# Gate columns stationary in four column groups, and attention values by pairs of heads, in a two-layer hybrid trunk

## The chip, the cores and the metric

The kernel runs on one core of one Trainium2 chip. The metric is the device time of one execution in microseconds (us), as the median of repeated runs. TensorE multiplies matrices into PSUM, VectorE, ScalarE and GpSimd work on elements, and SyncE issues most of the loads; the engines meet through semaphores.

## What is computed

Two groups of tokens, 512 latent tokens and 128 context tokens (640 in all), pass through the same two layers of width 1024. In each layer they are normalised and modulated, projected by `w_in`, go through three mixers, are projected by `w_out`, and then go through a routed set of 16 experts. Cut to what the change touches:

```python
p = modulated_norm(x, g_norm1[l], sh1, sc1) @ w_in[l]     # 640 x 1024 by 1024 x PROJ_W
glu, q_na, k_na, v_na, dn_qkv, dn_z, dn_ab = split_projection(p)

# dn_ab: the last 16 columns, gates of the delta mixer
ab = dn_ab.reshape(b, t, 4, DN_HEADS)
g = -exp(a_log) * softplus(ab[:, :, 0:2] + dt_bias)
beta = sigmoid(ab[:, :, 2:4])

# attention: 4 heads of 64; latent tokens see the latent grid (with a bias) and 128 cached context tokens
pr = softmax(concatenate([s_loc, s_ctx], axis=-1), axis=-1)
o = pr @ v          # context tokens see only context
```

All arrays are fp32.

## The kernel before

The kernel is written by hand: each engine has its own program, in the order in which the code is written, and every hand-over is a wait for a count on a semaphore (`need`). Activations lie transposed, features on the 128 partitions and the 640 tokens along the row: `hT` holds eight such tiles (index `k`). Weights come through a ring of three slots of 2 MB; SyncE loads the next piece into a slot when TensorE's last reader of that slot is done (`ring_load`, L518).

**Input projection (L685 to L706).** Seven pieces of `w_in` are worked off. A piece of 512 columns is four products (`gemm`), each of eight steps `k`, and each step of a matmul over 512 tokens (L680) and one over 128 (L681), with 128 weight columns stationary. After the fifth piece (`ci == 4`, the columns called Z) come the 16 gate columns (L704): for each of five blocks of 128 tokens, eight matmuls with the tokens stationary and the 16 weight columns `wab` moving. ScalarE copies them to `ab` (L1338) and makes `beta` (L1340); VectorE makes the gates from `ab` at L1715 to L1721. Then TensorE goes on with the sixth piece (Q and K of the attention, `ci == 5`) and the values of the attention (L692).

**Between projection and attention (L709 to L734).** A layer norm of the convolution mixer runs over TensorE (sums, L714 and L732), ScalarE (L1364, L1376) and VectorE (L1729, L1735, L1738); TensorE also transposes the cached keys, which ScalarE asks for at L1347 after the projection. GpSimd masks the table of attention biases in two operations (L2200, L2202), which VectorE's first attention step (L1753) waits for. In layer 0 GpSimd has stores of zeros (L2187) in its queue ahead of that; they begin when the Z product begins.

**Attention (L737 to L795).** Eighteen rounds: 16 for a block of 128 latent queries and one head, then two for the context tokens with two heads each. In round `i` TensorE transposes the probabilities (`turn_probs`, L760), makes the scores of round `i + 2` (`scores`, L745 and L746), multiplies the probabilities with the values (`values`, L775; L777 for the context rounds), and beside that works off a piece of `w_mod` (modulation for later): `mod_turn` (L639) and `mod_rows` (L633), which has 32 stationary columns in each of four column groups. Layer 0 has twelve such pieces (rounds 1 to 12 load rows, 2 to 13 turn), layer 1 eight. VectorE scales, takes the maximum and normalises (L1753 to L1772), ScalarE takes the exponentials (L1387), copies the transposed probabilities into one of two buffers `pT_` (L1401) and stores the head's result (`att_store`, L1409). A head's 64 outputs go to partitions 0 to 63 or 64 to 127, by the head's parity.

Of the kernel before, what the change touches and what calls it, by code (L numbers as in the profile page):

```python
# [12 lines left out]
P = 128  # L13
# [94 lines left out]
NC = C_SEL + 2  # L108
# [4 lines left out]
def constants():  # L113
# [37 lines left out]
    c[:, C_SEL:C_SEL + 2] = i[:, None] % 32 == np.arange(2)[None, :]  # L151
# [16 lines left out]
def build(nc, x_prompt, x_sample, cache_k, cache_v, state, c, c_ctx, w_mod, b_mod, g1, g2, w_in, conv_w,  # L168
# [11 lines left out]
    with ExitStack() as ctx:  # L180
# [24 lines left out]
        small = sb("small", [P, 1110 + 272])  # L205
# [8 lines left out]
        qkT = work[:, 0:4 * T].rearrange("p (t n) -> p t n", t=4)  # L214
        vna = work[:, 4 * T:4 * T + NCH * NAW].rearrange("p (t n) -> p t n", t=NCH)
# [24 lines left out]
        wab = carve(KD * 16).rearrange("p (k n) -> p k n", k=KD)  # L240
# [125 lines left out]
        ab_done = signal("ab_done", 1)  # L366
        ab_copied = signal("ab_copied", 1)
# [21 lines left out]
        att_o = signal("att_o", 20)  # L389
        att_oc = signal("att_oc", 20)  # L390
# [207 lines left out]
        def _(pe):  # L598
# [20 lines left out]
            for l in range(L):  # L619
# [66 lines left out]
                for ci, (o, w) in enumerate(IN_CHUNKS):  # L686
# [24 lines left out]
                need(ab_copied, 1)  # L711
# [51 lines left out]
                def values(i):  # L763
                    need(att_ptc, i + 1)
                    src = pT_[i % 2]
                    for h in ([i % 4] if i < 16 else [2 * (i - 16), 2 * (i - 16) + 1]):
                        u = i if i < 16 else h + 16
                        r = slice(64 * (h % 2), 64 * (h % 2) + 64)
                        o = ps[r, 3072:3072 + P]
                        if u >= 2:  # L770
                            need(att_oc, u - 1)
                        if i < 16:
                            for j in range(NCH):
                                va = vna[:, j, 64 * h:64 * h + 64] if j < 4 else kvc[1][:, 64 * h:64 * h + 64]
                                ins = mm(o, va, src[:, P * j:P * (j + 1)], start=j == 0, stop=j == NCH - 1)  # L775
                        else:
# [1558 lines left out]
```

## Time and profile before

| | us |
|---|---|
| median of 3 runs | 1985.38 (1984.87 to 1989.67) |
| the profiled execution | 1986.52 |
| its span, first to last instruction | 1984.7 |
| TensorE busy (matmul) | 1726.3 |
| VectorE busy | 856.5 |
| ScalarE busy | 473.9 |
| GpSimd busy | 287.3 |
| mean granted TensorE clock | 0.923 |

The profile is one execution, and its times count from its first instruction. An fp32 matmul shows as two passes, each with its own load of the stationary operand. A row of the timeline merges neighbours of one kind, with their count; in brackets stands the idle time of the engine before it and what ended that. In a row of stretches each engine has its busy time and its count, and behind them stand the granted clock (1.00 is 2.4 GHz, 0.50 is 1.2 GHz), the share of the DMA engines' time that was used, and GB/s.

### The profile page before, as it was taken

The page shows a single profiled execution, that of the slowest core. Times are in us where ns is not written, and L with a number is a line of the kernel's source. Part 1 is how long each engine was busy: PE and PEld are TensorE (multiplying, and loading weights), DVE is VectorE, ACT ScalarE, POOL GpSimd, SP SyncE. Part 2 cuts the span into 40 slices and gives each one's busy share as a digit, 9 for nine tenths or more (in the row PEclk, how much of TensorE's full clock was granted, in tenths as well). Part 3 has the DMA queues.
Part 4 walks back from the last instruction along what each step waited for, and adds up shares of the span by engine and source line. Part 5 has one row for each costly group of instructions (what it writes and reads, how often), then busy time and mean ns, then how long its engine had stood idle before and what let it go on. Part 6 is the DMA issues. An engine that isn't in the chain of part 4 may idle for free. (4 is left out here: it accounts for less than half of the span.)

```text
span 1984.7 us, 22021 instructions
## 1 busy us (share of the span) xinstructions
PE 1726.3 (87%) x8313; PEld 1109.2 (56%) x8313; DVE 856.5 (43%) x1631; ACT 473.9 (24%) x850; POOL 287.3 (14%) x446
## 2 busy tenths in 40 slices
PE   5999996977998895999689999797699989499994
PEld 3555663645887553455355556554488855344553
DVE  2188105556786323111246840254678632411115
ACT  1211003254231213222131110324522120311222
POOL 0000122014442003000211000000435200400002
PEclk9999896988999996999889998798899999699996
DMA  9511996920000106999571101380000010599974
GB/s 344 132 43 65 286 266 210 347 75 1 1 1 1 55 22 260 364 366 362 220 186 68 60 22 43 106 297 1 1 1 1 1 55 21 220 386 360 368 295 180
DMA packets 114392, 302.33 MB, mean 152 GB/s; under 512 B 28000, under 2 KB 36098, under 8 KB 101250
## 3 DMA queue, kind: packets, MB, share of 16 engines
q1 hardware_dynamic: 66576, 221.30, 30.1%
q0 software_dynamic: 14080, 53.48, 8.1%
q10 hardware_dynamic: 33650, 26.37, 4.7%
q8 instruction: 58, 0.95, 0.2%
q14 instruction: 28, 0.23, 0.0%
HBM read 235.04 MB, written 67.05 MB: 152 GB/s over the span
## 5 line engine op out<-in xcount | busy, mean ns | idle before, releaser
L680 PE MATMUL ps<-hreg,ring 128*128 128x512 f32 x768 | 401.7, 605 | 11.1 <-ACT hreg L1291 11.1
L681 PEld LDWEIGHTS ps<-hreg,ring 128*128 128x128 f32 x768 | 148.3, 193 | 188.5 <-issue 188.5
L1124 PE MATMUL ps<-ring,tok 128*128 128x512 f32 x544 | 237.9, 595 | 0.2 <-issue 0.2
L1124 PEld LDWEIGHTS ps<-ring,tok 128*128 128x128 f32 x544 | 103.9, 191 | 130.9 <-issue 130.9
L681 PE MATMUL ps<-hreg,ring 128*128 128x128 f32 x768 | 149.2, 276 | 0.0
L680 PEld LDWEIGHTS ps<-hreg,ring 128*128 128x128 f32 x768 | 119.0, 196 | 11.4 <-issue 11.4
L2126 DVE TENSOR_TENSOR work<-work,ps 128x256 f32<-128x256 f32 x34 | 14.2, 421 | 251.1 <-ACT work L1549 251.1
L1139 PE MATMUL ps<-ring,work 128*128 128x512 f32 x272 | 122.4, 592 | 0.0
L1685 DVE SCALAR_TENSOR_TENSOR mixA<-cin_reg,small,mixA 128x655 f32<-128x655 f32 x120 | 107.1, 896 | 0.0
L2130 DVE COPY zs<-ps 128x1024 f32<-128x1024 f32 x34 | 41.6, 1225 | 120.8 <-PE ps L1139 120.8
L2209 POOL TENSOR_TENSOR hreg<-dnT,cst 128x512 f32<-128x512 f32 x16 | 20.4, 1276 | 488.7 <-DVE dnT L1887 488.7
L1699 DVE SCALAR_TENSOR_TENSOR tmp_reg<-mixb_reg,small,tmp_reg 128x642 f32<-128x642 f32 x96 | 84.7, 882 | 0.0
L1139 PEld LDWEIGHTS ps<-ring,work 128*128 128x128 f32 x272 | 49.1, 191 | 48.8 <-issue 48.8
L2304 POOL DMA_INDIRECT hreg<-ys,slots x10 | 12.5, 1248 | 402.2 <-ACTq L1570 399.8
L1108 PE MATMUL ps<-cst,tok 128*128 128x128 f32 x304 | 43.8, 291 | 27.1 <-DMA tok<-hx,idx 27.1
L1045 PE MATMUL ps<-dnT,ring 128*128 128x512 f32 x128 | 65.5, 594 | 0.0
L1981 DVE SCALAR_TENSOR_TENSOR xT<-ps,small,xT 128x512 f32<-128x512 f32 x16 | 12.0, 751 | 105.9 <-PE ps L1046 105.9
L1326 ACT ACTIVATE mixb_reg<-ps 128x512 f32<-128x512 f32 x24 | 14.3, 598 | 174.0 <-PE ps L681 174.0
L1108 PEld LDWEIGHTS ps<-cst,tok 128*128 128x128 f32 x304 | 39.7, 196 | 28.0 <-issue 25.4
L1717 DVE SCALAR_TENSOR_TENSOR small<-small 128x40 f32<-128x40 f32 x2 | 1.9, 956 | 114.7 <-ACT small L1355 114.7
L1540 ACT ACTIVATE tok<-ps 128x1024 f32<-128x1024 f32 x38 | 38.9, 1025 | 51.7 <-PE ps L1108 48.0
L633 PE MATMUL ps<-ring,small 128*32 128x512 f32 x384 | 47.3, 614 | 3.8 <-issue 2.1
(351 smaller groups left out, 3003.4 us busy)
## 6 DMA issues: line engine op xcount, KB each, us to landing
ring<-in_w SPq DMA_DIRECT2D x102, 1024.0 KB, 7.6
ring<-in_w_mod SPq DMA_DIRECT2D x24, 2048.0 KB, 8.3
ring<-in_w_in SPq DMA_DIRECT2D x12, 2048.0 KB, 8.5
ys<-zs ACTq DMA_DIRECT2D x34, 512.0 KB, 7.7
tok<-xs SPq DMA_DIRECT2D x30, 512.0 KB, 10.7
xs<-zero POOLq DMA_DIRECT2D x8, 1792.0 KB, 19.7
ys<-zero POOLq DMA_DIRECT2D x8, 1664.0 KB, 18.6
ring<-in_w_out SPq DMA_DIRECT2D x4, 2048.0 KB, 7.9
```

The costliest lines, as they stand in the source:

```text
L633: ins = mm(bank(bnk)[32 * j:32 * j + 32], condT[:, k, :], w[:, k, :], start=k < 4, stop=k >= 4)
L680: mm(o[:, 0:TS], lhs(k), rhs(k)[:, 0:TS], start=k == 0, stop=k == nk - 1)
L681: ins = mm(o[:, TS:T], lhs(k), rhs(k)[:, TS:T], start=k == 0, stop=k == nk - 1)
L1045: mm(gslot(gg % 2)[:, 0:TS], lhs, mix(k)[0], start=k == 0, stop=k == KD - 1)
L1108: ins = turn(ps[:, a + P * k:a + P * (k + 1)], xg[q].rearrange("p (m k) -> p k m", k=KD)[:, k], ident)
L1124: ins = mm(bank(2 + q), xgT[q][:, k, :], w, start=k == 0, stop=k == KD - 1)
L1139: ins = mm(bank(4 + 2 * q + n), hidT[:, P * f:P * (f + 1)], ring[2][:, 2048 * q + D * f + 512 * n:2048 * q + D * f + 512 * n + 512], start ...
L1540: A_(xgT[q], ps[:, a:a + D].rearrange("p (k n) -> p k n", k=KD), ACT.Copy).then_inc(xg_copied.sem, 1)
L1685: last[t] = count(V.scalar_tensor_tensor(mixA[:, t, :], src, w, mixA[:, t, :], ALU.mult, ALU.add))
L1699: ins = V.scalar_tensor_tensor(out, src, w, out, ALU.mult, ALU.add)
L2130: V.tensor_copy(ysb[q], ps[:, 2048 + 1024 * q:3072 + 1024 * q]).then_inc(y_out.sem, 1)
L2209: G.tensor_tensor(rcos[t % 2], dnT[:, qk_tile(t), 0:TS], cst[:, C_COS:C_COS + TS], ALU.mult).then_inc(rope_cos.sem, 1)
```

## The change

Three things change.

The gate columns: the padded weight columns (16 and 16 zeros) are the stationary operand, in four column groups, and the tokens move. Group `k % 4` holds the sum over two of the eight steps, so the product lands as four partial sums of 16 rows (each at the start of 32 partitions). ScalarE copies that to `abr` (640 columns). One product later TensorE multiplies each block of 128 tokens of `abr` with a selector of 16 columns, which adds the four groups and turns tokens to partitions. `C_SEL` grows from 2 to 16 columns for that.

The values: `values(a)` runs for two heads at once, in rounds 1, 3, 5 and so on, and its matmuls alternate between partitions 0 to 63 and 64 to 127. One signal and one ScalarE store of 128 partitions serve both heads.

The order within a round: the modulation rows come straight after the scores, then the modulation's turns, then the values.

```diff
-NC = C_SEL + 2
+NC = C_SEL + 16
...
-    c[:, C_SEL:C_SEL + 2] = i[:, None] % 32 == np.arange(2)[None, :]
+    c[:, C_SEL:C_SEL + 16] = i[:, None] % 32 == np.arange(16)[None, :]
...
+        abr = work[:, 4 * T:5 * T]
...
-        wab = carve(KD * 16).rearrange("p (k n) -> p k n", k=KD)
+        wab = carve(KD * 32).rearrange("p (k n) -> p k n", k=KD)
...
                     for m in range(4):
+                        if ci == 5 and m == 1:
+                            need(pT_ready, 1)
+                            need(ab_copied, 1)
+                            for t in range(NCH):
+                                ins = mm(ps[:, 3584 + 16 * t:3600 + 16 * t], abr[:, t * P:(t + 1) * P], cst[:, C_SEL:C_SEL + 16],
+                                         start=True, stop=True)
+                            ins.then_inc(ab_done.sem, 1)
...
                     if ci == 4:
-                        need(pT_ready, 1)
-                        for t in range(NCH):
+                        for a, b in ((0, TS), (TS, T)):
                             for k in range(KD):
-                                ins = mm(ps[:, 3584 + 16 * t:3600 + 16 * t], hT[:, k, t * P:(t + 1) * P], wab[:, k, :],
-                                         start=k == 0, stop=k == KD - 1)
+                                j = 32 * (k % 4)
+                                ins = mm(ps[j:j + 32, 2048 + a:2048 + b], wab[:, k, :], hT[:, k, a:b], start=k < 4, stop=k >= 4)
                         ins.then_inc(ab_done.sem, 1)
...
+                def values(a):
+
+                    halves = [ps[64 * x:64 * x + 64, 3072:3072 + P] for x in range(2)]
+                    if a:
+                        need(att_oc, a)
+                    if a < 8:
+                        need(att_ptc, 2 * a + 2)
+                        for j in range(NCH):
+                            for x in range(2):
+                                h = 2 * (a % 2) + x
                                 va = vna[:, j, 64 * h:64 * h + 64] if j < 4 else kvc[1][:, 64 * h:64 * h + 64]
-                                ins = mm(o, va, src[:, P * j:P * (j + 1)], start=j == 0, stop=j == NCH - 1)
+                                ins = mm(halves[x], va, pT_[x][:, P * j:P * (j + 1)], start=j == 0, stop=j == NCH - 1)
...
-                    values(i)
-
+                    if 1 <= i < 1 + len(beside):
+                        if i >= 2:
+                            pe.wait_ge(mod_copied, beside[i - 2] + 1)
+                        mod_rows(beside[i - 1], 7)
                     if 2 <= i < 2 + len(beside):
+                        need(att_ptc, i + 1)
                         mod_turn(beside[i - 2], later_rows[i % 2], 2688 + 8 * (i - 2))
-                    if 1 <= i < 1 + len(beside):
-                        mod_rows(beside[i - 1], 7)
+                    if i >= 16 or i % 2:
+                        values(i // 2 if i < 16 else i - 8)
...
-                A_(ab, ps[:, 3584:3664].rearrange("p (c n) -> p c n", c=NCH), ACT.Copy).then_inc(ab_copied.sem, 1)
-                need(ab_copied, 1)
-                A_(beta, ab[:, :, 8:16], ACT.Tanh, scale=0.5)\
-                    .then_inc(beta_tanh.sem, 1)
+                A_(abr, ps[:, 2048:2048 + T], ACT.Copy).then_inc(ab_copied.sem, 1)
                 for t in range(4):
                     evac(G_QK + t, qkT[:, t, :]).then_inc(gemm_out[t % 2].sem, 1)
+                    if t == 0:
+                        need(ab_done, 2)
+                        A_(ab, ps[:, 3584:3664].rearrange("p (c n) -> p c n", c=NCH), ACT.Copy).then_inc(ab_copied.sem, 1)
+                        need(ab_copied, 2)
+                        A_(beta, ab[:, :, 8:16], ACT.Tanh, scale=0.5)\
+                            .then_inc(beta_tanh.sem, 1)
...
+                def att_store(a):
+                    need(att_o, a + 1)
+                    h, t = (a % 2, slice((a // 2) * P, (a // 2 + 1) * P)) if a < 8 else (a - 8, slice(TS, T))
+                    A_(mixB[:, h, t], ps[:, 3072:3072 + P], ACT.Copy).then_inc(att_oc.sem, 1)
...
                     if i + 1 < 18:
                         att_probs(i + 1)
+                    if i >= 2 and i % 2 == 0:
+                        att_store(i // 2 - 1)
+                    if i == 17:
+                        att_store(8)
                     att_copy(i)
...
+            V.memset(wab[:, :, 16:32], 0.0)
```

TensorE's program at the end of the Z columns in layer 0, before (`ps` is PSUM, `small` holds `wab`, `hreg` holds `hT`, `ring` the weights; a size is partitions by moving columns):

```order
L680 MATMUL ps<-hreg,ring 128x512
L681 MATMUL ps<-hreg,ring 128x128
L704 MATMUL ps<-small,hreg 128x16 [waits pT_ready]
L704 MATMUL ps<-small,hreg 128x16 x39
L680 MATMUL ps<-hreg,ring 128x512 [waits gemm_out0,ring_loaded2]
L681 MATMUL ps<-hreg,ring 128x128
```

and the same place after the change (`work` holds `abr`, `cst` the selector; "..." stands for the other steps of that product):

```order
L682 MATMUL ps<-hreg,ring 128x128
L712 MATMUL ps<-hreg,small 32x512 x8
L712 MATMUL ps<-hreg,small 32x128 x8
L681 MATMUL ps<-hreg,ring 128x512 [waits gemm_out0,ring_loaded2]
...
L682 MATMUL ps<-hreg,ring 128x128
L702 MATMUL ps<-cst,work 128x16 [waits ab_copied,pT_ready]
L702 MATMUL ps<-cst,work 128x16 x4
L681 MATMUL ps<-hreg,ring 128x512 [waits gemm_out1]
```

Forty matmuls in one run became sixteen, and five more stand behind the first product of the sixth piece.

TensorE's program for rounds 2 and 3 of the attention, before (`hreg` holds probabilities, cached keys and values, `work` Q, K and V, `tmp_reg` the modulation rows):

```order
L760 MATMUL ps<-cst,hreg 128x128 x4
L745 MATMUL ps<-work 128x512 [waits gemm_out0]
L746 MATMUL ps<-hreg,work 128x128
L775 MATMUL ps<-hreg,work 64x128 [waits att_oc,att_ptc]
L775 MATMUL ps<-hreg,work 64x128 x3
L775 MATMUL ps<-hreg 64x128
L639 MATMUL ps<-cst,tmp_reg 128x2 [waits mod_copied]
L639 MATMUL ps<-cst,tmp_reg 128x2 x3
L633 MATMUL ps<-ring,small 32x512 [waits ring_loaded2]
L633 MATMUL ps<-ring,small 32x512 x7
```

which is round 2, and round 3 reads alike. After the change round 2 ends with the turns, and round 3 reads:

```order
L767 MATMUL ps<-cst,hreg 128x128 [waits att_ptc,att_n]
L767 MATMUL ps<-cst,hreg 128x128 x4
L752 MATMUL ps<-work 128x512 [waits gemm_out1]
L753 MATMUL ps<-hreg,work 128x128
L634 MATMUL ps<-ring,small 32x512 [waits ring_loaded0,mod_copied]
L634 MATMUL ps<-ring,small 32x512 x7
L640 MATMUL ps<-cst,tmp_reg 128x2 [waits mod_copied,att_ptc]
L640 MATMUL ps<-cst,tmp_reg 128x2 x3
L781 MATMUL ps<-hreg,work 64x128 [waits att_ptc,att_oc]
L781 MATMUL ps<-hreg,work 64x128 x7
L781 MATMUL ps<-hreg 64x128 x2
```

The values of two rounds stand together, behind the modulation work instead of ahead of it.

## Rows read from the trace of the kernel before

**Rows 1.** Page, engines: busy us, share of the span, instructions.

```profile
PE 1726.3 (87%) x8313; PEld 1109.2 (56%) x8313; DVE 856.5 (43%) x1631; ACT 473.9 (24%) x850; POOL 287.3 (14%) x446
```

**Rows 2.** Timeline, layer 0's gate columns: start us, us, engine, line, operation, shapes, count.

```profile
228.30 13.85 PE L704 MATMUL ps<-small,hreg 128*128 128x16 f32 x80
...
241.98 2.06 PE L680 MATMUL ps<-hreg,ring 128*128 128x512 f32 x2
...
245.96 1.02 PE L680 MATMUL ps<-hreg,ring 128*128 128x512 f32 x2
...
247.04 1.02 PE L680 MATMUL ps<-hreg,ring 128*128 128x512 f32 x2
...
252.65 0.70 ACT L1306 ACTIVATE work<-ps 128x640 f32<-128x640 f32 x1 [9.96 <-PE ps L681]
```

**Rows 3.** Timeline, layer 1's gate columns.

```profile
1190.47 13.49 PE L704 MATMUL ps<-small,hreg 128*128 128x16 f32 x80
```

**Rows 4.** Stretch of layer 0's gate columns: PE, PEld, DVE, ACT, POOL, clock, DMA.

```profile
228.00:242.50 14.50, 14.50 (x84) 14.38 (x83) 0.05 (x1) 0.99 (x3) 4.54 (x3) 0.63 0.98 327
```

**Rows 5.** Timeline of TensorE, layer 0, attention round 2.

```profile
339.50 0.77 PE L760 MATMUL ps<-cst,hreg 128*128 128x128 f32 x5
...
341.47 1.09 PE L775 MATMUL ps<-hreg,work 128*64 128x128 f32 x8
...
342.71 1.05 PE L639 MATMUL ps<-cst,tmp_reg 128*128 128x2 f32 x8
...
343.69 1.92 PE L633 MATMUL ps<-ring,small 128*32 128x512 f32 x16
...
345.55 0.77 PE L760 MATMUL ps<-cst,hreg 128*128 128x128 f32 x5
```

**Rows 6.** Groups by line and shape: count, busy us, mean ns, idle before.

```profile
L775 PE MATMUL ps<-hreg,work 128*64 128x128 f32 x256 | 39.3, 303 | 0.9 <-ACT hreg L1401 0.7
...
L919 PE MATMUL ps<-ring,work 64*64 64x64 f32 x160 | 9.6, 224 | 0.0
```

**Rows 7.** Timeline, layer 0 between projection and attention; last, layer 1's L1719.

```profile
295.88 1.24 ACT L1345 ACTIVATE work<-ps 128x1280 f32<-128x1280 f32 x1 [16.56 <-PE ps L692]
...
301.96 6.87 POOL L2202 TENSOR_TENSOR tok<-tok,cst 128x3776 f32<-128x3776 f32 x1
301.98 6.91 DVE L1719 SCALAR_TENSOR_TENSOR small<-small 128x40 f32<-128x40 f32 x1
...
307.16 0.69 PE L721 MATMUL ps<-cst,hreg 128*128 128x128 f32 x2 [7.56 <-DMA hreg<-in_cache_na_v]
...
311.40 2.07 PE L732 MATMUL ps<-tmp_reg,cst 128*128 128x512 f32 x2 [3.13 <-ACT tmp_reg L1364]
...
317.67 1.01 DVE L1735 SCALAR_TENSOR_TENSOR mixA<-mixA,small,rst 128x512 f32<-128x512 f32 x2 [7.10 <-ACT rst L1377]
...
320.72 0.68 DVE L1753 SCALAR_TENSOR_TENSOR hreg<-ps,tok 128x512 f32<-128x512 f32 x1
...
1261.85 0.20 DVE L1719 SCALAR_TENSOR_TENSOR small<-small 128x40 f32<-128x40 f32 x1
```

**Rows 8.** Timeline of TensorE, layer 0, starts of attention rounds 0 and 1.

```profile
325.20 1.33 PE L760 MATMUL ps<-cst,hreg 128*128 128x128 f32 x5 [4.79 <-DVE hreg L1772]
...
331.64 1.33 PE L760 MATMUL ps<-cst,hreg 128*128 128x128 f32 x5 [0.36 <-DVE hreg L1772]
```

**Rows 9.** Stretches: layer 0's last rounds, a late round of layer 1, a middle round.

```profile
412.80:416.10 3.30, 3.30 (x16) 2.42 (x14) 0.85 (x4) 1.49 (x6) 0.00 (x0) 0.50 0.00 0
1345.54:1350.26 4.72, 3.27 (x19) 2.26 (x19) 2.49 (x6) 1.78 (x5) 0.00 (x0) 1.00 0.00 0
351.59:357.63 6.04, 6.04 (x47) 3.64 (x44) 3.18 (x7) 1.90 (x4) 0.00 (x0) 1.00 0.99 351
```

**Rows 10.** Line L518 (ring loads): time from issue to landing.

```profile
DMA to landing us min/median/max: 5.1/8.1/24.5
```

More of the change, by code:

```diff
@@ L204, in build @@
         work = sb("work", [P, 6 * T])
-        small = sb("small", [P, 1110 + 272])
+        small = sb("small", [P, 1110 + 400])
         rst = sb("rst", [P, T])[:, :]
@@ L365, in build @@
         dn_silu = signal("dn_silu", 12)
-        ab_done = signal("ab_done", 1)
-        ab_copied = signal("ab_copied", 1)
+        ab_done = signal("ab_done", 2)
+        ab_copied = signal("ab_copied", 2)
         v_done = signal("v_done", 1)
@@ L388, in build @@
         att_ptc = signal("att_ptc", 18)
-        att_o = signal("att_o", 20)
-        att_oc = signal("att_oc", 20)
+        att_o = signal("att_o", 10)
+        att_oc = signal("att_oc", 10)
         l2_sq = signal("l2_sq", 8)
@@ L761, in turn_probs @@
                     ins.then_inc(att_pt.sem, 1)
[L763 to L773, printed above, removed]
-                                va = vna[:, j, 64 * h:64 * h + 64] if j < 4 else kvc[1][:, 64 * h:64 * h + 64]
-                                ins = mm(o, va, src[:, P * j:P * (j + 1)], start=j == 0, stop=j == NCH - 1)
-                        else:
-                            ins = mm(o, vna[:, 4, 64 * h:64 * h + 64], src[:, P * (h % 2):P * (h % 2 + 1)], start=True, stop=True)
-                        ins.then_inc(att_o.sem, 1)
+                def values(a):
[7 more added lines that the diff above has]
+                                h = 2 * (a % 2) + x
+                                va = vna[:, j, 64 * h:64 * h + 64] if j < 4 else kvc[1][:, 64 * h:64 * h + 64]
+                                ins = mm(halves[x], va, pT_[x][:, P * j:P * (j + 1)], start=j == 0, stop=j == NCH - 1)
+                    else:
+                        need(att_ptc, a + 9)
+                        for x in range(2):
+                            h = 2 * (a - 8) + x
+                            ins = mm(halves[x], vna[:, 4, 64 * h:64 * h + 64], pT_[a % 2][:, P * x:P * (x + 1)], start=True, stop=True)
+                    ins.then_inc(att_o.sem, 1)
                 need(kc_copied, 1)
@@ L811, in _ @@
                 need(att_ptc, 18)
-                need(att_oc, 20)
+                need(att_oc, 10)
                 need(gemm_out[0], (G_CTX + 2) // 2)
@@ L1235, in load_params @@
                     (wr[:, :, 0:4], wg[l].rearrange("(k p) n -> p k n", p=P)),
[L1236 removed]
+                    (wab[:, :, 0:16], w_in[l][:, OFF_AB:PROJ].rearrange("(k p) n -> p k n", p=P)),
                     (wr[:, :, 4:20], we[l].rearrange("(k p) n -> p k n", p=P)),
@@ L1398, in att_copy @@
                     if i >= 2:
-                        need(att_o, i - 1)
+                        need(att_o, i // 2 if i < 17 else 9)
                     n = T if i < 16 else 2 * P
                     A_(pT_[i % 2][:, 0:n], ps[:, 2048:2048 + n], ACT.Copy).then_inc(att_ptc.sem, 1)
-                def att_store(i):
-                    for h in ([i % 4] if i < 16 else [2 * (i - 16), 2 * (i - 16) + 1]):
-                        u = i if i < 16 else h + 16
-                        need(att_o, u + 1)
-                        r = slice(64 * (h % 2), 64 * (h % 2) + 64)
-                        t = slice((i // 4) * P, (i // 4 + 1) * P) if i < 16 else slice(TS, T)
-                        A_(mixB[r, h // 2, t], ps[r, 3072:3072 + P], ACT.Copy).then_inc(att_oc.sem, 1)
+                def att_store(a):
+                    need(att_o, a + 1)
+                    h, t = (a % 2, slice((a // 2) * P, (a // 2 + 1) * P)) if a < 8 else (a - 8, slice(TS, T))
+                    A_(mixB[:, h, t], ps[:, 3072:3072 + P], ACT.Copy).then_inc(att_oc.sem, 1)
                 att_probs(0)
@@ L1710, in _ @@
                 ins.then_inc(conv_out.sem, 1)
-                need(ab_copied, 1)
+                need(ab_copied, 2)
                 row = dtb.rearrange("p (a n) -> p a n", a=1).to_broadcast([P, NCH, 8])
```

7 lines of the change are left out of this document (2 added, 5 removed).

## Prediction

> **What bounds the kernel now.** The page first: TensorE is busy 87% of the span, three other engines less than half [rows 1]. So the question at each place is whether TensorE is the engine that ends last there. I read three places of each layer. First the gate columns at L704: one uninterrupted run of 80 passes (an fp32 matmul shows as two passes in the trace, so 40 matmuls), 13.85 and 13.49 us long [rows 2, 3]. Nothing else is waited for, and the granted clock over the stretch is 0.63 [rows 4]: it began at 2.4 GHz and fell to 1.2 GHz while TensorE streamed 16 columns per pass. Second the attention loop, where in one round the transposes, scores, value products, modulation turns and modulation rows follow each other with no gap, 339.50 to 345.55, 6.05 us [rows 5], and a later one 6.04 [rows 9]: TensorE is the bound there too. Third the stretch between the input projection and the attention. There it is not: it waits for the cached keys and then for VectorE [rows 7].
>
> **Gate columns, at their own place.** Before, in layer 0, L704 takes 228.30 to 241.98, 13.68 us. The two steps of the next product, still at the low clock, take 241.98 to 245.96, 3.98 us, where two steps at the high clock take 2 x 1.08 (245.96 to 247.04), so 1.82 more [rows 2]. Together 15.5 us. Layer 1's run is 0.36 shorter [rows 3]; with the same tail 15.1.
> The change puts three groups in its place. Eight matmuls of 32 stationary columns and 512 moving ones, in four column groups: the modulation rows have this very shape, and take 343.69 to 345.55, 1.86 us [rows 5]. Eight of the same with 128 moving columns, 16 passes, are not in the trace. Their bounds are 60 ns a pass (L919's small passes, 9.6 us over 160) [rows 6] and 124 ns (ten value passes, 341.47 to 342.71) [rows 5], so 1.0 to 2.0 us; their 32 stationary columns are nearer to L919's 64 x 64, so I take 1.2. Five selector matmuls, ten passes with 128 stationary columns: the modulation turns have that shape, 8 passes in 0.98 (342.71 to 343.69), so 1.2 [rows 5]. Sum 4.3 us (4.1 to 5.1), and since the long streams are dense I expect no fall of the clock. Gain at the place: 11.2 us in layer 0, 10.8 in layer 1.
> The added ScalarE copy of 128x640 costs 0.70 and lies in an idle stretch of 9.96 us [rows 2]. TensorE waits for it only after one whole product (eight steps of 1.08), so its cover is 8 us; without the cover it would cost 0.7 twice. ScalarE's evacuations behind it start on TensorE's products, which come later. The memset of the padding stands at the program's start, where VectorE waits for the first loads; uncovered, some tenths. The larger constants are one wider load of the same kind.
>
> **What arrives in layer 1:** all 10.8. Its road into the attention has no load or GpSimd work that ends later than TensorE's products; VectorE's gate step L1719 takes 0.20 there [rows 7].
>
> **What arrives in layer 0:** less. GpSimd's second table operation L2202 stands at 301.96 to 308.83, and VectorE's L1719, a step of 40 columns, takes 6.91 us and ends at 308.89, with it [rows 7]. So VectorE stood still for a GpSimd operation. GpSimd's time does not hang on the gate columns: it follows its own zero stores, which start before them. After the change the products end 11.2 us earlier, at 284.7 for 295.88; the cached keys come 11.3 us after their issue (295.88 to 307.16), so 296.0; two pairs of transposes of 0.69; the variance chain, which took 311.40 to 317.67 [rows 7], 6.3 us, would then reach VectorE's L1735 at 303.7, inside L2202. L1735 has two operands in SBUF like L1719, so I let it wait until 308.9. From L1735 to the first attention step L1753 are 3.05 us (317.67 to 320.72), so the attention starts at 311.9 instead of 320.72: a gain of 8.8, and 2.4 are lost.
> The Trainium skill's page "SBUF — State Buffer", section "SBUF: two separate sides", states the rule: VectorE and GpSimd share a port pair under an exclusive lock, held for a whole instruction, and a VectorE operation with two SBUF inputs needs it. By that rule L1735 waits to 308.9; without it the gain would be 11.2; the trace agrees, with 6.91 us against 0.20.
>
> **Attention, middle rounds.** Values of two heads are now issued as 20 passes that alternate between output partitions 0 to 63 and 64 to 127. Before, ten passes of one head take 1.24, so two heads 2.48 [rows 5]. No row has two column groups of 64. Bounds: 2.48 if they don't overlap, and 1.2 at 60 ns a pass (L919) [rows 6]; the four-group rows (16 passes of 512 columns in 1.86, 116 ns each) against one group's 128 columns in 124 ns say that groups do run beside each other. I take 1.30. An round without values is 6.04 - 1.24 = 4.80, and with a pair 6.10. VectorE's chain allows that: in the last rounds, where TensorE idles, the period is 4.72 (1345.54 to 1350.26) [rows 9], just under 4.80. In layer 0, rounds 2 to 12 take 11 x 6.04 = 66.4, then 6 x 4.80 + 5 x 6.10 = 59.3: 7.1 gained. In layer 1, rounds 2 to 8: 42.3, then 4 x 4.80 + 3 x 6.10 = 37.5: 4.8 gained. Iteration 1 only trades one head's values at the low clock for a pair after the rows; I take nought (one either way). The new waits in it (turns wait for the probabilities' copy, rows for the copy of the rows before) are for work of 0.7 us on ScalarE and VectorE with 1.86 us of rows or a whole round between; behind them on TensorE stand only that round's own values.
> The skill's page "TensorE: Matmul & The Clock Gate", Part 3, gives 2.38 times for three column groups. As an estimate from that page a pair would take 2.48 / 1.59 = 1.56, and the sum would be 2 us less; the rows above it stand for more overlap than that.
>
> **Attention, last rounds.** In layer 1, rounds 10 to 15 have no modulation work and run at 4.72, TensorE busy 3.27 of it at clock 1.00 [rows 9]. Making the values cheaper saves nothing here, since VectorE's chain sets the period. But the idle of TensorE is regrouped: an even round keeps only transposes and scores, 1.97 (339.50 to 341.47) [rows 5], and idles 2.75. Busy time falls from 3.27 to 2.6 on average. The end of layer 0's loop, with short products, had the clock at 0.50 (412.8 to 416.1) [rows 9], so I expect it to fall here. An round at the low clock is 6.44 (325.20 to 331.64) [rows 8], so 1.72 more, for the transposes and scores are on VectorE's chain. Between none and all six I take three: 5.2 lost. Layer 0 has hardly any such rounds: 0.5 lost.
> ScalarE's half as many stores (one of 128 partitions for two of 64) are hidden under TensorE; uncovered they would save, not cost.
>
> **Sum.** 8.8 + 10.8 + 7.1 + 4.8 - 5.2 - 0.5 = 25.8 us. The profiled execution took 1986.52 with a span of 1984.7; the median of the runs, 1985.38, is 1.1 lower. 1986.5 - 25.8 = 1960.7 for an execution like the profiled one, 1959.6 for the median. Forecast 1959.5.
>
> **Rivals.**
> *The clock holds in the last rounds.* For it: 1.00 held there with 1.45 us idle in each. Then 5.7 come back: 1954. The clock gate page's section "Why this matters for your kernels" warns only of idle gaps longer than these; by that rule this rival would win, and no row here has gaps of just this kind. Chance 0.18.
> *The two halves don't overlap*, so the pair does not do what it is meant to. A pair then costs 2.48, an odd round 7.28; layer 0's middle is 65.2 (1.2 gained), layer 1's 41.0 (1.3): 9.4 less, 1969. Against it stand the four-group rows. Chance 0.13.
> *A load ends last.* Layer 0's cached keys may land at 307.16 whenever they are issued, since zero stores fill the queues: then 7.7 us of chain end at 314.9 for 317.67, 2.8 gained instead of 8.8: 1965. Or the modulation weights: 0.99 of the DMA time is used in an round of 6.04 [rows 9], and the mean round is to be 5.45. A load lands 8.1 us after its issue [rows 10] and is needed 3 x 5.45 - 1.86 = 14.5 after it, a lead of 6.4; nine loads use up 9 x 0.59 = 5.3. It just holds; if not, some 4 us. Chance 0.08.
> *Slower: alternating halves serialise*, each pass holding TensorE for its full recorded 303 ns [rows 6] instead of 124. A pair is then 6.1, 4.8 over my 1.30: ten pairs on the path (eight middle, two first) cost 48, five late odd rounds 3.3 each more: 65 lost against 26, some 2024. It decides from about 0.175 us a pass (a pair of 3.5). Against it: four groups alternate in the modulation rows without it. Chance 0.04.
>
> **How the numbers follow.** Forecast 0.55. Within 0.3% (about what a measurement of this kernel can tell from no change, 6 us) 0.02, slower 0.04, faster 0.94. Range 1949 to 1971: below it the warm tail together with an unpinned layer 0 (2.4), above it no overlap with a late load.
>
> **What would show it.** The gate passes near 4 us and clock 1.00 after them; the attention of layer 0 starting at 312, right after GpSimd's table; rounds of 4.8 and 6.1 by turns; pairs near 1.3; layer 1's last rounds between 4.72 and 6.44. Wrong if pairs take over 2 us, if TensorE waits for ring loads, or if an even middle round waits for VectorE.

## The result, and the profile after

The changed kernel takes 1957.76 us (median of four runs, 1952.31 to 1960.51), beside 1986.03 for the kernel before on the same chip: a ratio of 0.9851, 95% interval 0.9825 to 0.9877. The forecast was 1959.5, faster. The profiled execution of the changed kernel has a span of 1957.1 us, against 1984.7: 27.6 less, where the sum of the prediction was 25.8.

The page's line on the engines, for [rows 1] (busy us, share of the span, instructions):

```profile
PE 1688.2 (86%) x8237; PEld 1068.2 (55%) x8237; DVE 856.9 (44%) x1632; ACT 471.9 (24%) x832; POOL 287.1 (15%) x446
```

TensorE lost 38.1 us of busy time, the other engines next to nothing: what the kernel gained is TensorE's, less what it now waits.

The gate columns first. In the timeline of TensorE, layer 0 (start us, us, engine, line, operation, shapes, count), the two lines that stand for [rows 2]:

```profile
228.73 2.36 PE L712 MATMUL ps<-hreg,small 128*32 128x512 f32 x32
...
231.02 1.12 PE L681 MATMUL ps<-hreg,ring 128*128 128x512 f32 x2
...
239.78 1.19 PE L702 MATMUL ps<-cst,work 128*128 128x16 f32 x10
...
240.81 1.10 PE L681 MATMUL ps<-hreg,ring 128*128 128x512 f32 x2
```

L712 holds both sizes, 16 passes of 512 columns and 16 of 128; the next line starts 2.29 us after it. The selector passes L702 hold TensorE for 1.03. That is 3.3 us for 15.5, and the steps behind are at the high clock from the first one on (1.12, where [rows 2] have 2.06 and then 1.02). The stretch, to be laid beside [rows 4] (TensorE, its weight loads, VectorE, ScalarE, GpSimd, clock, DMA share, GB/s), has a granted clock of 1.00 for 0.63:

```profile
228.70:242.80 14.10, 14.10 (x81) 7.93 (x81) 0.20 (x1) 2.59 (x5) 4.48 (x3) 1.00 0.98 329
```

Then the start of layer 0's attention, the timelines of GpSimd, VectorE and TensorE, for [rows 7, 8]:

```profile
296.45 6.88 POOL L2214 TENSOR_TENSOR tok<-tok,cst 128x3776 f32<-128x3776 f32 x1
303.41 7.21 POOL L2216 TENSOR_TENSOR tok<-tok,cst 128x3776 f32<-128x3776 f32 x1
...
298.56 12.21 DVE L1749 SCALAR_TENSOR_TENSOR mixA<-mixA,small,rst 128x512 f32<-128x512 f32 x2 [8.07 <-ACT rst L1391]
...
311.28 1.01 DVE L1749 SCALAR_TENSOR_TENSOR mixA<-mixA,small,rst 128x512 f32<-128x512 f32 x2
...
312.80 0.68 DVE L1767 SCALAR_TENSOR_TENSOR hreg<-ps,tok 128x512 f32<-128x512 f32 x1
...
317.27 1.33 PE L767 MATMUL ps<-cst,hreg 128*128 128x128 f32 x5 [16.75 <-DVE hreg L1786]
```

L1749 is the L1735 of before. Two of its instructions, 1.01 us together a moment later, take 12.21 here: the first ends 0.56 behind GpSimd's L2214 (303.89 and 303.33), the second 0.15 behind L2216 (310.77 and 310.62). The first attention step starts at 312.80 for 320.72, and TensorE idles 16.75 us ahead of round 0, where it idled 4.79.

The attention's rounds, TensorE in layer 0, one odd round and the start of an even one, for [rows 5]:

```profile
336.66 0.75 PE L767 MATMUL ps<-cst,hreg 128*128 128x128 f32 x5
...
341.45 1.09 PE L781 MATMUL ps<-hreg,work 128*64 128x128 f32 x16
342.37 0.39 PE L781 MATMUL ps<-hreg 128*64 128x128 f32 x4
342.69 0.77 PE L767 MATMUL ps<-cst,hreg 128*128 128x128 f32 x5
...
347.43 0.75 PE L767 MATMUL ps<-cst,hreg 128*128 128x128 f32 x5
```

The pair's 20 passes L781 hold TensorE from 341.45 to 342.69, 1.24 us, as long as one head's ten did before. The odd round is 6.03 (336.66 to 342.69), the even one 4.74 (342.69 to 347.43).

Last, three late rounds of layer 1 in the stretches, for the middle row of [rows 9]:

```profile
1307.70:1312.42 4.72, 2.04 (x9) 1.20 (x9) 2.48 (x6) 1.79 (x5) 0.00 (x0) 1.00 0.00 0
1312.42:1318.10 5.68, 5.32 (x30) 3.49 (x30) 2.48 (x6) 1.64 (x4) 0.00 (x0) 0.58 0.01 3
1318.10:1324.53 6.43, 3.75 (x9) 2.09 (x9) 2.48 (x6) 1.78 (x5) 0.00 (x0) 0.50 0.00 0
```

In round 10 TensorE is busy 2.04 of 4.72 us; then the clock falls, and rounds 11 to 13 take 5.67, 6.44 and 6.44.

Where the 27.6 us came from, by the starts of the attention's transposes (first number: when round 0 starts; the loop is from there to round 17):

| | before | after | gained |
|---|---|---|---|
| layer 0: start of round 0 | 325.20 | 317.27 | 7.9 |
| layer 0: loop | 94.4 | 86.4 | 7.9 |
| from there to layer 1's round 0 | 858.5 | 846.5 | 12.0 |
| layer 1: loop | 90.5 | 90.3 | 0.3 |
| from there to the end | 616.0 | 616.6 | -0.6 |

### The profile page after: what moved, and what is told of

It reads as the page before. It is cut to its first block and busy times, and to the rows that moved or that the text cites. A ratio compares the mean times of both kernels' runs of the same rounds, so it can differ in the third digit from the quotient of the medians.

```text
span 1957.1 us, 21878 instructions
## 1 busy us (share of the span) xinstructions
PE 1688.2 (86%) x8237; PEld 1068.2 (55%) x8237; DVE 856.9 (44%) x1632; ACT 471.9 (24%) x832; POOL 287.1 (15%) x446
## 5 line engine op out<-in xcount | busy, mean ns | idle before, releaser
L681 PE MATMUL ps<-hreg,ring 128*128 128x512 f32 x768 | 397.7, 600 | 11.1 <-ACT hreg L1303 11.1
L767 PE MATMUL ps<-cst,hreg 128*128 128x128 f32 x168 | 30.8, 320 | 38.9 <-DVE hreg L1786 38.9
L1120 PEld LDWEIGHTS ps<-cst,tok 128*128 128x128 f32 x304 | 39.9, 197 | 27.1 <-issue 26.5
L1767 DVE SCALAR_TENSOR_TENSOR hreg<-ps,tok 128x512 f32<-128x512 f32 x32 | 22.1, 690 | 72.3 <-PE ps L753 72.3
```

Of the source, the lines that this page charges most:

```text
L681: mm(o[:, 0:TS], lhs(k), rhs(k)[:, 0:TS], start=k == 0, stop=k == nk - 1)
L767: ins = turn(ps[:, 2048 + P * j:2048 + P * (j + 1)], sc[i % 2][:, P * j:P * (j + 1)], ident)
L1120: ins = turn(ps[:, a + P * k:a + P * (k + 1)], xg[q].rearrange("p (m k) -> p k m", k=KD)[:, k], ident)
L1767: V.scalar_tensor_tensor(s[:, 0:TS], o[:, 0:TS], HD ** -0.5, Tz[:, b * GRID:b * GRID + TS], ALU.mult, ALU.add)
```

## The experiments

Eleven more runs followed; e5 is the kernel before once more. For each, the median, the ratio to the kernel before with its 95% interval, and from its profile the start of layer 0's round 0, both loops, and rounds 9 to 13 of layer 1 (23.6 us if all five take 4.72):

| | us (runs) | ratio | L0 start | L0 loop | L1 loop | 9 to 13 |
|---|---|---|---|---|---|---|
| before | 1986.03 (4) | | 325.20 | 94.4 | 90.5 | 23.6 |
| changed | 1957.76 (4) | 0.9851 (0.9825 to 0.9877) | 317.27 | 86.4 | 90.3 | 28.0 |
| e1 gate alone | 1961.5 (4) | 0.9894 (0.986 to 0.9928) | 316.76 | 90.6 | 92.4 | 27.4 |
| e2 attention alone | 1979.89 (12) | 0.9973 (0.9956 to 0.9989) | 326.88 | 90.4 | 88.3 | 27.0 |
| e3 gate in order | 1959.25 (4) | 0.9872 (0.9845 to 0.99) | 316.91 | 86.5 | 90.5 | 30.2 |
| e4 pairs in order | 1963.17 (4) | 0.9889 (0.9861 to 0.9918) | 316.60 | 93.3 | 91.2 | 28.2 |
| e5 before again | 1991.35 (1) | | 327.02 | 94.6 | 90.7 | 25.8 |
| e6 late split | 1949.34 (4) | 0.9824 (0.9802 to 0.9845) | 318.02 | 85.8 | 85.9 | 26.5 |
| e7 table early | 1948.63 (5) | 0.9825 (0.9806 to 0.9844) | 303.78 | 87.3 | 90.6 | 30.1 |
| e8 filled | 1946.2 (5) | 0.9812 (0.979 to 0.9834) | 316.97 | 83.1 | 83.8 | 27.0 |
| e9 gate, one group | 1980.1 (1) | | 327.23 | 87.5 | 90.6 | 30.2 |
| e10 early and filled | 1930.0 (5) | 0.9731 (0.9717 to 0.9744) | 307.28 | 84.8 | 80.3 | 23.7 |
| e11 the same, late split | 1933.0 (5) | 0.9743 (0.9728 to 0.9758) | 307.73 | 83.5 | 80.3 | 23.7 |

A ratio is taken to executions of the kernel before that ran beside it, and these differed a little from set to set (medians 1984.2 to 1986.0). So where two rows of the table are compared, the difference is given by the medians and by the ratios; they can be some 4 us apart.

### The two parts apart

e1 is the changed kernel with the values, the order within a round and the stores of before; e2 is the kernel before with these three changed and its own gate columns.

> The gate part alone; the attention is that of the kernel before. My theory: the gate stage takes 3.4 us (32 passes in about 2.3, ten selector passes in about 1.2) for 13.7, layer 0's attention starts at 312.8 for 320.7 (7.9 gained; VectorE's step before it is held by GpSimd's table), layer 1 gains 12, rounds stay at 6.04 and layer 1's late ones at 4.72 with clock 1.00. Sum 20 us: 1966, ratio 0.990. Rival, that part of the 12 in layer 1 comes from an attention of layer 0 with other clocks or loads: less than 10 in layer 1.

> The attention part alone; the gate columns are those of the kernel before. My theory: rounds of 4.74 and 6.03 by turns in both layers, layer 0's loop 8 us shorter; in layer 1 five us gained in the middle and five lost in the last rounds, whose period is 5.7 to 6.4 at the low clock. Sum 8.2 us: 1977.5, ratio 0.9959. Rival, that the late rounds fall only because of something that the gate part shifts: then they hold 4.72, and the gain is 13 us: 1972.5.

e1's gate rows are those of the changed kernel (2.36 and 1.19), its first attention step is at 312.28, and its rounds are 6.04. Its ratio of 0.9894 is 21 us, beside 20 expected. e2 has rounds of 4.74 and 6.03 or 6.04 by turns; its ratio is 5 us, with an interval that holds the 8 expected. The two ratios multiply to 0.9867, against 0.9851 for the whole, 3 us apart and inside the intervals: as far as these runs can tell, the parts add. From layer 0's loop to layer 1's start the three kernels with the old gate columns (before, e5, e2) take 854.7 to 859.4 us, and the eight with four column groups in turn (changed, e1, e4, e6 to e8, e10, e11) 841.6 to 846.5. So the 12.0 of layer 1 is the gate's, give or take 3.

But e1 brought a surprise. Its attention has the old order, and still its late rounds in layer 1 are 4.72, 4.72, 5.10, 6.44 and 6.44. In e2 two of them are 6.44. So the fall there needs neither the pairs nor the gate part.

### What makes the column groups fast

e3 lets two steps after each other go to one column group, so that four passes in a row share it; e9 gives all steps to one group.

```diff
-                                j = 32 * (k % 4)
-                                ins = mm(ps[j:j + 32, 2048 + a:2048 + b], wab[:, k, :], hT[:, k, a:b], start=k < 4, stop=k >= 4)
+                                j = 32 * (k // 2)
+                                ins = mm(ps[j:j + 32, 2048 + a:2048 + b], wab[:, k, :], hT[:, k, a:b], start=k % 2 == 0, stop=k % 2 == 1)
```

```diff
...
+                                ins = mm(ps[0:32, 2048 + a:2048 + b], wab[:, k, :], hT[:, k, a:b], start=k == 0, stop=k == KD - 1)
...
```

(In e9 the selector and the copy to `abr` take 32 partitions, too.)

> The changed kernel, but two steps after each other go to one column group (0, 0, 1, 1, 2, 2, 3, 3) where before four groups took turns; same matmuls, same sums. If column groups run beside each other only when the next pass goes to another group, the 32 passes take up to 9.6 us in place of 2.3 (16 x 0.48 and 16 x 0.12), with two of one group in a row some 5. Layer 1 then loses all of that, 3 to 7 us, layer 0 almost nothing, since its attention's start is held by GpSimd's table to 310.8: 1961 to 1965. Rival, that the small number of stationary columns is what makes them fast: no change, 2.3 us and 1958.

> The changed kernel, but all eight steps of the gate columns go to one column group, partitions 0 to 31, and the selector sums 32 partitions for 128; same stationary and moving sizes. Theory (the four column groups make the passes overlap, whatever their order): without groups a 512-column pass takes 0.43 us and a 128-column pass 0.11 as in the products around it, the stage 8.7 us for 2.3. Layer 1 loses 6.3 us; layer 0 nothing, since its attention waits for GpSimd's table until 310.7: 1964. Rival (few stationary columns alone make it fast): 2.4 us again, 1958.

The timeline of TensorE, first e3 and then e9:

```profile
228.68 2.40 PE L712 MATMUL ps<-hreg,small 128*32 128x512 f32 x32
```

```profile
229.91 8.80 PE L711 MATMUL ps<-hreg,small 128*32 128x512 f32 x32
```

In e3 nothing changes, and my expectation falls: the groups need not take turns from pass to pass. Without groups the same passes take 8.80 us, 3.7 times 2.36. So the groups are what makes them fast, and not the few stationary columns.

e9 missed in layer 0, where I expected no loss. Its attention starts 10.0 later than the changed kernel's, for a gate stage of 6.4 more; 1.2 of that lie ahead of it already (GpSimd's first store starts at 196.08 for 194.90). Layer 1 lost 6.0 (852.5 for 846.5), as expected. The rows of VectorE tell why:

```profile
295.79 8.20 DVE L1730 SCALAR_TENSOR_TENSOR small<-small 128x40 f32<-128x40 f32 x1 [46.50 <-ACT small L1368]
304.02 6.90 DVE L1732 SCALAR_TENSOR_TENSOR small<-small 128x40 f32<-128x40 f32 x1
...
319.71 1.02 DVE L1748 SCALAR_TENSOR_TENSOR mixA<-mixA,small,rst 128x512 f32<-128x512 f32 x2 [7.11 <-ACT rst L1390]
```

With the later gate it is again the two steps of 40 columns that meet GpSimd's table, as in the kernel before. They stand at the head of a chain of 8.9 us (310.84 to 319.71), while L1749 stands at its end. What GpSimd's table costs depends on which VectorE step it meets.

### Pairs that don't alternate

```diff
-                        for j in range(NCH):
-                            for x in range(2):
+                        for x in range(2):
+                            for j in range(NCH):
```

> The changed kernel, but a pair's value products are issued head after head: ten passes for partitions 0 to 63, then ten for 64 to 127. If the gain comes from alternation, a pair takes 2.48 us for 1.29 and an odd middle round 7.2 for 6.03: seven such rounds in layer 0 and four in layer 1, 13 us lost, less up to 5 that come back if the busier TensorE keeps its clock in layer 1's last rounds: 1966 to 1971. Rival, that the gain comes from half as many stores and waits: odd rounds stay at 6.03, 1958.

Odd rounds take 6.74 us, between the two: 0.71 are lost and not 1.2. The time is 5 us over the changed kernel's by the medians and 8 by the ratios, where 8 to 13 were expected. The timeline of TensorE in one of them:

```profile
341.90 1.14 PE L781 MATMUL ps<-hreg,work 128*64 128x128 f32 x10
342.83 0.27 PE L781 MATMUL ps<-hreg 128*64 128x128 f32 x1
342.88 0.27 PE L781 MATMUL ps<-hreg,work 128*64 128x128 f32 x1
342.94 0.27 PE L781 MATMUL ps<-hreg 128*64 128x128 f32 x1
342.99 0.71 PE L781 MATMUL ps<-hreg,work 128*64 128x128 f32 x5
343.54 0.38 PE L781 MATMUL ps<-hreg 128*64 128x128 f32 x2
343.85 0.77 PE L767 MATMUL ps<-cst,hreg 128*128 128x128 f32 x5
```

The pair takes 1.95 us (341.90 to 343.85). In the middle of it passes start 0.05 to 0.06 apart, where the first head's last passes and the second head's first ones run side by side; before and after that they start 0.11 apart. By the records the second head's first three passes start ahead of the first head's last one: of the ten passes in the first line, eight are the first head's and two the second's. If a pass can get ahead of a few others only, that would explain why ten in a row for one head cost time and four in a row to one group (e3) did not; no run varies that number alone. Alternation brings the pair from 1.95 to 1.24, and the rival, that only the stores and waits count, is out.

### The late rounds and the clock

e5 is the kernel before, profiled a second time. e6 issues the values head by head in the rounds without modulation work:

```diff
...
-                    if i >= 16 or i % 2:
+                    if i < 16 and i // 2 * 2 >= 2 + len(beside):
+                        one_head(i // 2, i % 2)
+                    elif i >= 16 or i % 2:
```

> The kernel before, unchanged, for a second profiled execution. The gate part alone, with the attention's order unchanged, had late rounds of 5.1, 6.44 and 6.44 us in layer 1, though the first profile of before has 4.72 five times. Theory A, that these rounds stand at the edge and the clock falls in some executions of either order: a second execution may show one to three rounds of 5 to 6.44 among them, its time 2 to 5 us over the profiled one. Theory B, that they fall only in changed kernels: 4.72 five times again.

> The changed kernel, but in the rounds without modulation work (10 to 15 of layer 1, 14 and 15 of layer 0) the values are issued head by head again, one head in each round, so that TensorE's idle time is spread as in the kernel before. My theory of the prediction (pairing regroups the idle time, so the clock falls): rounds 9 to 13 of layer 1 go back to 4.72 at clock 1.00, 4.9 us gained, 1953. Rival (the gate part alone had falls in that order too): some of these rounds still take 5 to 6.44, and the gain is 0 to 3 us.

e5 decides for theory A. Late rounds of the unchanged kernel, in the stretches:

```profile
1342.93:1347.64 4.71, 3.27 (x19) 2.25 (x19) 2.48 (x6) 1.89 (x5) 0.00 (x0) 1.00 0.00 0
1347.64:1352.57 4.93, 4.57 (x19) 3.29 (x20) 2.48 (x6) 1.79 (x5) 0.00 (x0) 0.67 0.00 0
1352.57:1359.01 6.44, 6.08 (x19) 4.09 (x20) 2.48 (x6) 1.90 (x5) 0.00 (x0) 0.50 0.00 0
```

The same instructions that ran at 1.00 in the first profile run here at 0.67 and 0.50, with TensorE idle for 1.45 us in the round ahead. Of these two executions the first was the lucky one in these rounds. By the last column of the table, values head by head there (before, e5, e1, e6) give 23.6, 25.8, 27.4 and 26.5, a mean of 25.8; pairs in turn (changed, e3, e7, e9, e2) give 28.0, 30.2, 30.1, 30.2 and 27.0, a mean of 29.1. So both orders lose rounds to the low clock, and in the mean of nine profiles pairs lose some 3 us more, though the two groups touch (27.4 and 27.0). e6 gains 4.3 us in layer 1's loop (85.9 for 90.3), and its time is 8 us under the changed kernel's by the medians, 5 by the ratios. But of the 4.3 only 1.5 lie in rounds 9 to 13; 2.0 lie in rounds 14 to 16, and 0.9 in rounds 0 and 1, which the edit leaves as they were. Its late rounds are not all back at 4.72 (5.58, 6.44 and 5.06 among them). So my theory falls as far as e6 goes, and the rival (0 to 3 us) holds; that pairs lose more rests on the nine profiles alone.

e8 adds products that nobody reads, to keep TensorE at work:

```diff
+                def fill(n):
+                    for _ in range(n):
+                        mm(ps[:, 3584:3968], ones, cst[:, C_COS:C_COS + 384], start=True, stop=True)
...
+                fill((10, 4)[l])
...
+                    if i == 0:
+                        fill(2)
+                    if 1 + len(beside) <= i < 16:
+                        fill(1 if i % 2 else 3)
```

> The changed kernel with extra products on TensorE whose result nobody reads (ones by 384 constant columns, some 0.64 us each at 2.4 GHz): ten (layer 0) and four (layer 1) before the first attention round, two in round 0, and one or three in each round without modulation work. Nothing is left out. My theory (the clock falls since TensorE pauses): rounds 9 to 13 of layer 1 take 4.72 at clock 1.00 (4.9 us gained), and rounds 0 and 1 of both layers 4.7 to 5.0 and 6.0 to 6.5 instead of 6.44 and 8.2 to 9.3 (some 4 us a layer): 12 us, 1946. Rival, that the clock does not hang on TensorE's own work: rounds as before, or longer by the products: 1958 to 1968.

1946.2, as expected in sum (12 us under the changed kernel by the medians, 8 by the ratios), but not by place. Rounds 0 and 1 together take 11.6 and 11.7 for 14.7 and 15.7, so 3.1 and 4.0 come from there (round 0 stays at 6.44, round 1 falls to 5.11 and 5.24). The late rounds 9 to 13 gain 1.0 only: round 9 takes 7.06 and round 10 5.74, and then three of 4.72 follow. Where the clock fell, in the stretches:

```profile
1292.90:1296.30 3.40, 3.40 (x26) 2.58 (x22) 1.80 (x6) 1.63 (x3) 0.00 (x0) 1.00 0.90 337
1296.30:1299.70 3.40, 3.40 (x27) 3.05 (x27) 2.10 (x6) 1.03 (x3) 0.00 (x0) 0.51 0.09 33
```

TensorE had not paused at all: 3.40 of 3.40 us busy. It had done the turns of the modulation, which stream two columns, the transposes and the scores. That is like the gate columns of before, which streamed 16 columns without a pause when the clock fell [rows 4]. In the changed kernel the same turns stand in rounds 2 to 12 of layer 0, with modulation rows of 512 columns beside them, and there the clock is 1.00 throughout (331.92 to 390.50). Which part of this makes the clock fall, no run varies alone.

### GpSimd's table earlier

```diff
...
+                    if rows_ is xs and n == 3:
+                        mask_table(0)
             for l in range(L):
...
+                if l:
+                    mask_table(l)
```

> The changed kernel, but layer 0's two table operations of GpSimd stand after the first four of its sixteen zero stores, in its idle stretch of 25 us, and no longer behind the last. My theory (VectorE's step with two SBUF operands is held by them from 298.56 to 310.77): that step takes 1.0 us instead of 12.2, the attention of layer 0 starts at 306 instead of 317.3, 11.2 us gained, 1947; VectorE's convolution steps at 201 to 216 are held instead, and have 36 us of slack. Rival, that another wait (cached keys, ring loads, the low clock) ends last there: 0 to 4 us gained.

The timelines of GpSimd and VectorE:

```profile
199.93 6.88 POOL L2205 TENSOR_TENSOR tok<-tok,cst 128x3776 f32<-128x3776 f32 x1
206.89 7.36 POOL L2207 TENSOR_TENSOR tok<-tok,cst 128x3776 f32<-128x3776 f32 x1
...
197.10 10.42 DVE L1699 SCALAR_TENSOR_TENSOR mixA<-cin_reg,small,mixA 128x655 f32<-128x655 f32 x1
207.44 7.49 DVE L1713 SCALAR_TENSOR_TENSOR tmp_reg<-mixb_reg,small,tmp_reg 128x642 f32<-128x642 f32 x1
...
296.26 1.01 DVE L1749 SCALAR_TENSOR_TENSOR mixA<-mixA,small,rst 128x512 f32<-128x512 f32 x2 [7.38 <-ACT rst L1391]
...
299.31 0.68 DVE L1767 SCALAR_TENSOR_TENSOR hreg<-ps,tok 128x512 f32<-128x512 f32 x1
```

L1749 takes 1.01 for 12.21, and the first attention step is at 299.31 for 312.80: 13.5 earlier, of which 1.6 lie ahead of it already (GpSimd's first store starts at 193.27 for 194.90), so 11.9 where 11.2 were expected. The hold has gone to where the table went: two convolution steps take 10.42 and 7.49 for 0.9 each, and 36 us of slack swallow it. So the hold cost 11.9 us at this place. The whole time is 9 us under the changed kernel's by the medians and 5 by the ratios, whose intervals overlap.

In e7 the first held step begins at 197.10, ahead of GpSimd's operation at 199.93. GpSimd's issuing of stores is not what held it: in the changed kernel a step of the same line, in the midst of the same four issues, takes 0.90 us, and so do its neighbours.

```profile
194.90 6.55 POOL L2201 DMA_DIRECT2D xs<-zero  x4 [194.46 <-PE ps L682]
...
197.10 0.90 DVE L1699 SCALAR_TENSOR_TENSOR mixA<-cin_reg,small,mixA 128x655 f32<-128x655 f32 x1
```

### Both together

e10 has the early table and extra products: six ahead of round 0, two in round 0, one ahead of each layer's last modulation turns, one or three in the later rounds. e11 has the late values head by head besides, with two products in each late round.

> Table early and extra products together: layer 0's table of GpSimd in its idle stretch, six extra products before the first attention round of either layer, two in round 0, one ahead of the last turns of layer 1's modulation rows (round 9), one or three in the later rounds. My theory: the attention of layer 0 starts at 304 to 306 (11 to 13 us gained over the changed kernel, as with the table alone), rounds 0 and 1 take 5 to 6.4 and 5.2, layer 1's late rounds 4.72 to 5 with a fall in at most two of them: both gains add, some 9 from the table and 11 from the clock, 1937. Rival, that the two share their gain, since with a shorter wait the clock falls less before round 0 anyway: 1942 to 1945.

> As the kernel before this one in the list, and the rounds without modulation work issue their values head by head, with two extra products in each. My theory: the clock holds as there, so that it does not matter how the values are spread: within 2 us of that kernel, 1935 to 1939. Rival, that the even spread is what holds the clock: the late rounds stay at 4.72 here and fall there, 3 to 5 us less than that kernel.

e10 takes 1930.0 us, where 1937 were expected: 28 less than the changed kernel by the medians and 24 by the ratios; e7 and e8 alone gave 9 and 12 by the medians, 5 and 8 by the ratios. By place the two gains add: layer 0's round 0 starts 10.0 earlier (13.5 in e7; GpSimd's stores begin 1.5 later than in the changed kernel here and 1.6 earlier there), and the two loops are 11.6 shorter (9.9 in e8), 21.6 for 23.4. Inside the loops it came out otherwise than expected. Round 1 still takes 7.95 and 6.71, where I expected 5.2. The late rounds, which e8 had not mended, take 4.72 to 4.82, at clock 1.00; e10 has one product ahead of the last turns, where e8 has none, but no run changes that alone. Two of them, even and odd:

```profile
1290.43:1295.16 4.73, 4.18 (x18) 2.26 (x16) 2.49 (x6) 1.79 (x5) 0.00 (x0) 1.00 0.00 0
1295.16:1299.88 4.72, 4.12 (x32) 2.56 (x32) 2.48 (x6) 1.62 (x4) 0.00 (x0) 1.00 0.00 0
```

e11 has the same 23.7 in rounds 9 to 13. So with TensorE kept at work it does not matter in those rounds how the values are spread. The loops of e11 are as short as e10's or shorter (its rounds 0 and 1 take 9.8 in both layers, the first profile in which they do), but rounds 14 to 16 take 9.7 for 8.1. Both kernels issue four products in rounds 14 and 15; but head by head the values take 1.2 us in each of the two, where e10's pair takes 1.24 once, and TensorE waits for ScalarE's copy in both (0.46 and 0.37). Its time is 3 us more than e10's by the medians, with intervals that overlap.

## Why the prediction was right

**Gate columns at their place.** Forecast 4.3 us of TensorE (bounds 4.1 to 5.1), measured 3.3. The mis-sized term is the 128-column group, taken as 1.2 us of its own: both groups together take 2.29, so it adds 0.43 to the 1.86 of the 512-column passes. Its lower bound of 60 ns a pass, from L919, was not low enough (0.43 over 16 passes is 27 ns): those passes have 64 stationary columns, these 32, in four groups. That the dense streams keep the clock at 1.00 was right.

**Layer 1:** 10.8 forecast, 12.0 measured; the term above is most of the difference.

**Layer 0:** 8.8 forecast, 7.9 measured, and the mechanism was the one named: VectorE's step with two SBUF operands is held until GpSimd's second table operation ends, and e7 removes the hold with the table. The term that was off is the table's own time: it ends at 310.62, 1.8 later than before (308.83). GpSimd's stores began 0.3 later in this execution and came 0.3 to 0.5 further apart each, and the second operation took 7.21 for 6.87. That last part is no accident: it took 7.21 in all six kernels where a 512-column step of VectorE got through ahead of it (changed, e1, e3, e4, e6, e8), and 6.87 in the four where steps of 40 columns met the table (before, e2, e5, e9). From the hold's end to the first attention step are 2.0, where I had counted 3.05.

What I had wrong is the price of the hold: 2.4 us in the prediction, 11.9 in e7. By my own chain the attention would have started at 303.7 + 3.05 without it, a gain of 14.0 and not 11.2, for the kernel before lost time to the same table [rows 7]. And VectorE came to the step at 298.56, not 303.7: the keys took 8.1 us from their issue for 11.3, and the chain behind them 6.1 for 7.7. The hold ends last either way, so it is luck that none of this shows in the forecast.

The Trainium skill's page "SBUF — State Buffer", section "SBUF: two separate sides", gives the rule of an exclusive lock for the length of one instruction; the trace agrees on that length in three places, with 12.21 us for two instructions in the changed kernel, 10.42 and 7.49 in e7, and 8.20 and 6.90 in e9. In each case one VectorE instruction got through between the two operations of GpSimd.

**Middle rounds.** Pair 1.30 forecast, 1.24 measured from first pass to the next line; rounds 4.80 and 6.10 forecast, 4.74 and 6.03 measured. Layer 0's rounds 2 to 12 gained 7.85 for 7.1, layer 1's rounds 2 to 8 5.2 for 4.8. In e4, without alternation, an even and an odd round take 11.48 together, for 12.08 before and 10.77 changed: alternation gives 0.71 of the 1.31, and most of the rest comes with the two heads side by side in the middle of the pair (1.95 for 2.48).

**Last rounds.** The loss came out as forecast, 4.9 for 5.2 (rounds 9 to 16), but by luck, for the step behind it was half wrong. I read the first profile's 1.00 in these rounds as a property of the old order [rows 9], and put the whole fall down to the pairs. e5 and e1 show that the old order falls too, by 2.2 and 3.8 us; the pairs' own share is some 3 us in the mean, and from profile to profile rounds 9 to 13 of the pairs took 27.0 to 30.2. I also counted six late rounds at 4.72, where there are five (9 to 13). The rival that the clock holds, which I had tied to the advice of the Trainium skill's page "TensorE: Matmul & The Clock Gate", section "Why this matters for your kernels", against long idle gaps, is out: here the clock fell behind idle times of 1.45 us (e5) and 2.68 us (changed kernel), and in e8 behind none. Layer 0's last rounds gained 0.4, where I had taken 0.5 off.

**The other rivals.** That the halves don't overlap or that they serialise fell with the pair of 1.24. No load ended last: layer 0's keys landed 8.1 us after their issue (284.32 to 292.42), and the middle rounds waited for nothing.

**Sum:** 7.9 + 12.0 + 7.9 + 5.2 - 4.9, with 0.4 lost in the first rounds, 0.4 gained in layer 0's last ones and 0.6 lost behind the loops, is 27.5 for 25.8.

## What to carry to other kernels

When one engine's operation holds another engine, a shorter chain ahead of the hold is worth only what the hold leaves: look for the holder's own idle time and move it there (11.9 us at the place, 5 to 9 in the whole time here). Put small products into different column groups (2.36 us for 8.80 in one group), alternating from pass to pass where each group has many of them (1.24 us for 1.95). A granted clock of 1.00 in one profile of a thinly used stretch is no promise: profile the kernel twice before counting on it, and price it at both levels.

## What was not expected of the hardware

- A pass for another column group can start ahead of passes that were issued before it (e4: three of them). Four in a row to one group cost nothing (2.40 us for 2.36); ten in a row made a pair 0.71 longer (1.95 for 1.24).
- The clock can fall with TensorE busy without a pause (3.40 of 3.40 us in e8, 14.50 of 14.50 in [rows 4]); among its passes just before were turns of 2 columns in the one place, and gate passes of 16 in the other. And the same instructions ran at 1.00 in one execution and at 0.50 in another (before, e5).
- VectorE's held steps began before GpSimd's operation did by the records: 2.8 us ahead in e7 (197.10 and 199.93) and 1.25 in e9 (295.79 and 297.04), while GpSimd was still issuing the stores ahead of it. The issue alone does not hold VectorE: in the changed kernel steps of the same line took 0.90 us while GpSimd issued stores. GpSimd's spans are rough, so when its operation really took hold stays open.
- Work that computes nothing paid: the extra products added TensorE time and, together with the early table, took 28 us off by the medians (24 by the ratios), where the table alone took 9 (5).
